# A Mamba-2 mixer's group loop: product banks evacuated into SBUF, its queues reordered

## The chip, the cores and the metric

The kernel runs on one core of a Trainium2 chip as one program. The time is the device time in microseconds. The core's engines are TensorE (PE: matmuls, PEld: its weight loads), VectorE (DVE), ScalarE (ACT), GpSimd (POOL) and SyncE (SP, which only issues transfers). Each works through its own queue of instructions in order; between engines they wait on semaphores. TensorE reads from SBUF and writes to the eight banks of PSUM, 128 partitions of 512 fp32 numbers each.

## The reference

Three blocks on 512 tokens of width 1024, all in fp32: a block with a short convolution and an FFN, a block with a Mamba-2 mixer and an FFN, and a block of windowed and sparse attention with an FFN. The change touches the mixer alone:

```python
z, xbc, dt_raw = split(h @ w_in)
xbc = silu(causal_depthwise_conv(xbc, conv_w) + conv_b)          # width 4
xs, bm, cm = split(xbc)                                           # 8 groups
dt = softplus(dt_raw + dt_bias);  a = -exp(a_log)
y = ssd(xs, dt, a, bm, cm) + d_skip * xs
y = rms_normalize_per_group(y * silu(z)) * norm_g
return y @ w_out
```

`ssd` is, for each head, y_t = C_t h_t with h_t = exp(dt_t a) h_(t-1) + dt_t B_t x_t^T. A group has 4 heads of 64 columns, and B and C of 128 columns that its heads share.

## The kernel before

Every large product is made in three matmuls of single-pass fp32 pieces: a weight chunk of 128x1024 is loaded into one of 4 ring slots (`raw`), ScalarE rounds it to its high part (`whi`, L1103), GpSimd subtracts to get the low part (`wlo`, L514), and TensorE multiplies high by high, high by low and low by high (L553). A chunk is 24 matmuls of 128x512.

The mixer runs group by group. While group g is scanned, the projections of group g + 1 run. The scan takes its quadratic form: with S the running sums of dt times a, the product for a head is (C B^T, masked, times exp(S_l - S_s)) times (dt x). One round of the loop, `m_body(g)`, holds on each engine:

- TensorE: six projection chunks of group g + 1; between them `ssd_turn` (8 transpositions of x, banks 4 and 5), `ssd_sum` (the sum of squares over the partitions for the norm of group g - 1, by a product with ones, bank 7), `ssd_cb` (C B^T, banks 4, 5 and 6) and `ssd_y` twice (half f = 0 into bank 7, f = 1 into bank 6).
- VectorE: `conv` of the four parts of group g + 1 (s = 0, 1 for x, 2 for B, 3 for C; four operations each, L1721 and L1723), `scaled_x` (dt x, L1908), `group_sum` (adds the squares of the two halves, L1891), `segment` (S_l - S_s cut at 0, L1918), `masked_cb` (L1924), `decayed` (exponential times C B^T, L1933), `group_norm` (reciprocal L1896, two products L1898) and `epilogue` (adds D x, L1882, and multiplies with silu(z), L1886) for each half.
- ScalarE: `split_next` (the roundings L1103), `ssd_exp` (three exponentials L1273 and one L1275 for each head), `copy_cb` (the copies L1282 and L1283 out of banks 5 and 6), `group_root` (L1291), `conv_silu` (L1257: xg twice, bg, cg), `gate_silu` (L1263) and `group_square` (L1287). Exponential, root and silu each need another table, so that a change between them is a table load.

The order on each engine is the order in which these calls stand in the code; nothing moves them. `grp_ready` counts the silu results of a group's four parts, `y_done` the products of `ssd_y`, `yt_done` the finished halves of the epilogue, `gacc` the added squares, `gsum` their sum on TensorE, `gstd` the roots, `cbm_act` the copies.

Behind the seventh round stands the last group, written out: while it is scanned, TensorE begins the output product `m_out` from the groups that are normalized already (`out_high`, `out_low`, `out_part`). ScalarE and VectorE split each normalized tile into `m_hi` (L1330) and `m_lo` (L1564), in the calls `mixed(first, last)`.

## Time and profile before

| | |
|---|---|
| time, median of 3 runs | 2211.74 us (2209.34 to 2215.78) |
| the profiled execution's own time | 2215.78 us |
| its span, from the first to the last instruction | 2213.9 us |
| TensorE busy | 2173.9 us, 98% |
| VectorE busy | 1200.6 us, 54% |
| ScalarE busy | 999.4 us, 45% |
| GpSimd busy | 972.5 us, 44% |
| TensorE's granted clock, mean | 0.983 |

The busy time of an engine is the union of its instructions. Matmuls are pipelined: each row's duration (0.39 us for a 128x512 one) is longer than the distance between two starts, so the starts tell more than the durations. An idle time in brackets names who released the instruction.

### The profile page before, as it was taken

Reading aid. Unit: us, or ns where it says so; the run is one execution under the profiler, and the core shown is the slowest. Engines: PE = TensorE matmul, PEld = TensorE weight load, DVE = VectorE, ACT = ScalarE, POOL = GpSimd, SP = SyncE. Lnnn points to the kernel's source line nnn. Section 1 sums busy time; section 2 is a strip of 40 time slices with the busy share of each in tenths; the row PEclk is TensorE's granted clock in tenths of the full one; section 3 lists DMA queues with packets and bytes.
Section 4 is the critical chain, followed back from the end, with each engine's and each line's share of the span. In section 5 each row is a group of like instructions: output and inputs, shape, how many; then the busy total and the mean of one; then the engine's idle time right before and its main releaser. Section 6 shows DMA issues by size and latency. Waiting matters only on the chain.

```text
span 2213.9 us, 29018 instructions
## 1 busy us (share of the span) xinstructions
PE 2173.9 (98%) x10458; PEld 1762.6 (80%) x10458; DVE 1200.6 (54%) x1719; ACT 999.4 (45%) x1425; POOL 972.5 (44%) x421
## 2 busy tenths in 40 slices
PE   7999999999999999999999999999999999999998
PEld 5788888888878777778888888888777688888886
DVE  5876665521176877876522221240888745666512
ACT  4324543334445655654543434453555644444432
POOL 3544444346644333334544456556122143444563
PEclk8999999999999999999999999999999899999999
DMA  7653475553315344333233223344221132333232
GB/s 316 220 209 124 159 275 204 189 155 96 119 49 192 115 147 157 114 124 103 69 99 100 93 76 94 108 122 156 85 70 45 33 105 81 107 97 95 78 95 74
DMA packets 74337, 273.88 MB, mean 124 GB/s; under 512 B 8631, under 2 KB 11319, under 8 KB 67848
## 3 DMA queue, kind: packets, MB, share of 16 engines
q1 hardware_dynamic: 70872, 266.77, 36.4%
q10 hardware_dynamic: 3376, 5.90, 0.8%
q8 instruction: 58, 0.95, 0.2%
q14 instruction: 31, 0.25, 0.0%
HBM read 269.24 MB, written 8.12 MB: 125 GB/s over the span
## 4 chain that ended last, share of the span: by engine, by line
PE 76%; issue 13%; POOL 5%; DVE 4%; ACT 1%; DMA 1%; ACTq 0%; SPq 0%; POOLq 0%; DVEq 0%
PE bank L553 60%; POOL wlo L514 5%; PE bank L973 4%; PE bank L1065 2%; PE bank L576 1%; PE bank L1030 1%; PE bank L994 1%; PE bank L618 1%; PE bank L1013 1%; PE bank L626 1%; PE bank L580 1%; PE bank L665 1%; DMA ada_first<-ada_d 1%; DVE x L1623 1%; DVE bank L1686 1%
## 5 line engine op out<-in xcount | busy, mean ns | idle before, releaser
L514 POOL TENSOR_TENSOR wlo<-raw,whi 128x1024 fp32r<-128x1024 f32 x382 | 927.0, 2434 | 1150.0 <-ACT whi L1103 1149.7
L1103 ACT ACTIVATE whi<-raw 128x1024 fp32r<-128x1024 f32 x382 | 400.6, 1055 | 560.4 <-PE bank L553 537.0
L553 PE MATMUL bank<-h_hi,whi 128*128 128x512 f32 x1608 | 633.0, 394 | 1.9 <-POOL wlo L514 1.9
L553 PE MATMUL bank<-h_hi,wlo 128*128 128x512 f32 x1608 | 626.5, 390 | 0.0
L553 PE MATMUL bank<-h_lo,whi 128*128 128x512 f32 x1608 | 625.8, 389 | 0.0
L553 PEld LDWEIGHTS bank<-h_hi,whi 128*128 128x128 f32 x1608 | 301.9, 188 | 68.0 <-issue 6.3
L553 PEld LDWEIGHTS bank<-h_hi,wlo 128*128 128x128 f32 x1608 | 301.8, 188 | 64.3
L553 PEld LDWEIGHTS bank<-h_lo,whi 128*128 128x128 f32 x1608 | 302.0, 188 | 61.5
L553 PE MATMUL bank<-g_hi,whi 128*128 128x512 f32 x592 | 230.4, 389 | 0.0
L553 PE MATMUL bank<-g_hi,wlo 128*128 128x512 f32 x592 | 230.3, 389 | 0.0
L553 PE MATMUL bank<-g_lo,whi 128*128 128x512 f32 x592 | 230.3, 389 | 0.0
L1785 DVE TENSOR_TENSOR tb<-ta,bank 128x512 f32<-128x512 f32 x44 | 30.2, 686 | 210.1 <-PE bank L553 193.4
L1564 DVE TENSOR_TENSOR g_lo<-tb,g_hi 128x512 f32 (+1 forms) x52 | 108.2, 2081 | 51.9 <-ACT g_hi L1235 45.0
L553 PEld LDWEIGHTS bank<-g_lo,whi 128*128 128x128 f32 x592 | 111.1, 188 | 23.2
L553 PEld LDWEIGHTS bank<-g_hi,whi 128*128 128x128 f32 x592 | 111.1, 188 | 23.0
L553 PEld LDWEIGHTS bank<-g_hi,wlo 128*128 128x128 f32 x592 | 111.1, 188 | 23.0
L1580 DVE TENSOR_TENSOR sums<-sums,sq 128x512 f32<-128x512 f32 x21 | 14.5, 692 | 186.2 <-ACT sq L1166 186.1
L1723 DVE SCALAR_TENSOR_TENSOR tb<-bank,vec,tb 128x511 f32<-128x511 f32 (+1 forms) x140 | 104.9, 749 | 9.8
L576 PE MATMUL bank<-h_hi,whi 128*128 128x512 f32 x160 | 67.2, 420 | 10.4 <-ACT h_hi L1148 10.4
L529 POOL TENSOR_TENSOR h_lo<-tb,h_hi 128x512 fp32r<-128x512 f32 x35 | 45.2, 1293 | 67.2 <-ACT tb L1149 66.8
L576 PE MATMUL bank<-h_hi,wlo 128*128 128x512 f32 x160 | 66.2, 414 | 0.0
L2153 DVE TENSOR_TENSOR x<-x,bank 128x512 f32<-128x512 f32 x8 | 5.5, 688 | 86.4 <-PE bank L553 86.4
(359 smaller groups left out, 2994.5 us busy)
## 6 DMA issues: line engine op xcount, KB each, us to landing
raw<-f_in_d SPq DMA_DIRECT2D x88, 512.0 KB, 3.5
raw<-m_d SPq DMA_DIRECT2D x65, 512.0 KB, 3.6
ada_f<-ada_d SPq DMA_DIRECT2D x24, 1024.0 KB, 6.7
raw<-g_in_d SPq DMA_DIRECT2D x44, 512.0 KB, 3.5
raw<-w_in_d SPq DMA_DIRECT2D x41, 512.0 KB, 3.5
csb<-cs_d SPq DMA_DIRECT2D x32, 640.0 KB, 6.1
ada_a<-ada_d SPq DMA_DIRECT2D x16, 1024.0 KB, 4.9
raw<-a_in_d SPq DMA_DIRECT2D x24, 512.0 KB, 5.9
```

What stands on the lines that cost most here:

```text
L514: nc.gpsimd.tensor_tensor(wlo[:, s], raw[:, s], whi[:, s].bitcast(F32), ALU.subtract).then_inc(lo_ready, 1)
L529: nc.gpsimd.tensor_tensor(h_lo[:, k, :], tb[:, k % 2, :], h_hi[:, k, :].bitcast(F32), ALU.subtract).then_inc(in_ready, 1)
L553: mm = nc.tensor.matmul(psum[bank][:], w[:, s, kk, :], xs[part == "lo"][:, k, :], start=first and kk == 0 and i == 0, stop=last and kk == ...
L576: nc.tensor.matmul(psum[tiles[i]][:], w[:, (C0[name] + i) % RING, k, :], h_hi[:, k, :], start=k == 0 and j == 0, stop=False)
L580: mm = nc.tensor.matmul(psum[tiles[i]][:], whi[:, (C0[name] + i) % RING, k, :], h_lo[:, k, :], start=False, stop=k == KD - 1)
L618: mm = nc.tensor.matmul(psum[bank][:, i:i + 1], src[:, i * P:(i + 1) * P], ones[:, 0:1], start=start and i == 0, stop=False, skip_group_ch ...
L973: mm = nc.tensor.matmul(psum[7][:], w[:, c % RING, m // 3, :], (h_hi, h_lo)[part == "lo"][:, m // 3, :], start=m == 0, stop=m == 23)
L1065: mm = nc.tensor.matmul(psum[b][:], w[:, c % RING, k, :], (h_hi, h_lo)[part == "lo"][:, k, :], start=kk == 0 and i == 0, stop=kk == 3 and ...
L1103: nc.scalar.activation(whi[:, s], raw[:, s], ACT.Copy).then_inc(hi_ready, 1)
L1564: TT(dst, whole, hi.bitcast(F32), ALU.subtract).then_inc(in_ready, 1)
L1723: ins = STT(out=out[:, d:S], in0=src[:, 0:S - d], scalar=col(width - 1 - d), in1=out[:, d:S], op0=ALU.mult, op1=ALU.add)
L1785: TT(tb[:, j % 2, :], ta[:, j % 2, :], psum[b][:], ALU.mult).then_inc(bank_free[b], 1)
```

## The change

The second operand of the epilogue changes its place: its first operation writes into `ta` in SBUF instead of back into the PSUM bank, and a new semaphore `y_evac` counts it; TensorE waits for `y_evac` where it waited for `yt_done` before it writes banks 6 and 7 again. `ssd_turn` waits for all four parts of the next group, where it waited for two and `ssd_cb` for the rest. The last group's sum of squares goes into bank 6 (`group_bank`), as one product over squares that VectorE has added, where TensorE had added them in two products. On ScalarE and VectorE several calls change places. The diff, without its first hunk that only declares the semaphore:

```diff
--- before
+++ after
@@ -276,6 +276,10 @@
             sem(n) for n in ("score_done", "soft_done", "pexp_done", "pn_done", "tr_done", "pt_done", "pv_done"))
 
         block = ctx.enter_context(nc.Block())
+
+        def group_bank(g):
+
+            return 7 if g < GROUPS - 1 else 6
 
         def tile(t, j):
 
@@ -741,11 +745,11 @@
             def ssd_sum(g):
 
                 pe.wait_ge(gacc, g + 1)
-                nc.tensor.matmul(psum[7][:], ones[:], sq[:, 0, :], start=True, stop=True).then_inc(gsum, 1)
+                nc.tensor.matmul(psum[group_bank(g)][:], ones[:], sq[:, 0, :], start=True, stop=True).then_inc(gsum, 1)
 
             def ssd_turn(g, p):
 
-                pe.wait_ge(grp_ready, 4 * g + 2)
+                pe.wait_ge(grp_ready, 4 * (g + 1))
                 for f in range(2):
                     for i in range(NT):
                         mm = nc.tensor.transpose(psum[4 + f][:, i * P:(i + 1) * P], xg[:, p, f, i * P:(i + 1) * P], ident)
@@ -754,7 +758,6 @@
             def ssd_cb(g, p):
 
                 pe.wait_ge(xdt_done, 2 * (g + 1))
-                pe.wait_ge(grp_ready, 4 * (g + 1))
                 for i in range(NT):
                     nc.tensor.matmul(psum[4][:, i * P:(i + 1) * P], bg[:, p, i * P:(i + 1) * P], cg[:, p, i * P:(i + 1) * P],
                                      start=True, stop=True)
@@ -773,7 +776,7 @@
                 if f:
                     pe.wait_ge(cbm_act, 2 * (g + 1))
                 elif g:
-                    pe.wait_ge(yt_done, 2 * g - 1)
+                    pe.wait_ge(y_evac, 2 * g - 1)
                 bank = psum[7 - f]
                 for i in range(NT):
                     for off in range(1 + (i in OFF_COL)):
@@ -798,7 +801,7 @@
                 project(1)
                 if g:
                     ssd_sum(g - 1)
-                    pe.wait_ge(yt_done, 2 * g)
+                    pe.wait_ge(y_evac, 2 * g)
                 ssd_cb(g, p)
                 project(2)
                 project(3)
@@ -874,7 +877,7 @@
             ssd_turn(g, g % 2)
             out_high(1)
             ssd_sum(g - 1)
-            pe.wait_ge(yt_done, 2 * g)
+            pe.wait_ge(y_evac, 2 * g)
             ssd_cb(g, g % 2)
             out_high(2)
             for m in range(3):
@@ -885,10 +888,7 @@
             ssd_y(g, 1)
             out_part(0, near - 2, near)
             out_part(1, CH, near)
-            for f in range(2):
-                pe.wait_ge(gsq_out, 2 * g + f + 1)
-                mm = nc.tensor.matmul(psum[7][:], ones[:], sq[:, f, :], start=f == 0, stop=f == 1)
-            mm.then_inc(gsum, 1)
+            ssd_sum(g)
             out_part(2, CH, near)
             out_part(3, CH, near)
             for m in range(4):
@@ -1288,18 +1288,20 @@
 
             def group_root(g):
                 act.wait_ge(gsum, g + 1)
-                nc.scalar.activation(rstd[:], psum[7][:], ACT.Sqrt, bias=epscol[:], scale=1.0 / 256).then_inc(gstd, 1)
+                nc.scalar.activation(rstd[:], psum[group_bank(g)][:], ACT.Sqrt, bias=epscol[:], scale=1.0 / 256).then_inc(gstd, 1)
 
             def m_body(g):
 
                 G = g + 1
+                if g:
+                    group_square(g - 1, 1)
                 split_next(G, 0)
                 ssd_exp(g, 0)
-                copy_cb(g)
                 ssd_exp(g, 1)
                 split_next(G, 1)
                 if g:
                     group_root(g - 1)
+                copy_cb(g)
                 ssd_exp(g, 2)
                 ssd_exp(g, 3)
                 conv_silu(G, 0)
@@ -1317,11 +1319,9 @@
                     return
                 group_square(g, 0)
                 conv_silu(G, 3)
-                gate_silu(G, 0)
-                split_next(G, 4)
-                group_square(g, 1)
-                gate_silu(G, 1)
-                split_next(G, 5)
+                for f in range(2):
+                    gate_silu(G, f)
+                    split_next(G, 4 + f)
 
             def mixed(first, last):
 
@@ -1346,9 +1346,9 @@
             copy_cb(g)
             ssd_exp(g, 2)
             ssd_exp(g, 3)
+            mixed(8, 12)
+            group_root(g - 1)
             split_hi(C0["m_out"] + RING)
-            group_root(g - 1)
-            mixed(8, 12)
             split_hi(C0["m_out"] + RING + 1)
             mixed(12, 14)
             split_hi(C0["m_out"] + RING + 2)
@@ -1879,11 +1879,12 @@
 
                 p = g % 2
                 dve.wait_ge(y_done, 2 * g + f + 1)
-                step(STT(out=psum[7 - f][:], in0=xg[:, p, f], scalar=V("m_d", 2 * g + f), in1=psum[7 - f][:],
-                         op0=ALU.mult, op1=ALU.add))
+                STT(out=ta[:, f, :], in0=xg[:, p, f], scalar=V("m_d", 2 * g + f), in1=psum[7 - f][:],
+                    op0=ALU.mult, op1=ALU.add).then_inc(y_evac, 1)
+                dve.wait_ge(y_evac, 2 * g + f + 1)
 
                 read_out(T0["m_in"] + 1 + GSTEP * g + 4 + f)
-                TT(ta[:, f, :], psum[7 - f][:], zg[:, p, f], ALU.mult).then_inc(yt_done, 1)
+                TT(ta[:, f, :], ta[:, f, :], zg[:, p, f], ALU.mult).then_inc(yt_done, 1)
 
             def group_sum(gi):
 
@@ -1945,15 +1946,15 @@
                     scaled_x(g)
                 segment(g, 0)
                 segment(g, 1)
+                conv(G, 1)
                 masked_cb(g)
                 decayed(g, 0)
                 decayed(g, 1)
-                conv(G, 1)
                 segment(g, 2)
                 segment(g, 3)
+                conv(G, 2)
                 decayed(g, 2)
                 decayed(g, 3)
-                conv(G, 2)
                 if g:
                     group_norm(g - 1)
                 conv(G, 3)
@@ -1980,13 +1981,14 @@
             decayed(g, 1)
             segment(g, 2)
             segment(g, 3)
+            mixed(8, 12)
             decayed(g, 2)
             decayed(g, 3)
-            mixed(8, 12)
             group_norm(g - 1)
             mixed(12, 14)
             for f in range(2):
                 epilogue(g, f)
+            group_sum(g)
             group_norm(g)
             mixed(14, 16)
             residual_sums("m_out", 2, y_m, sums_m)
```

Two places show the new order. The first is on ScalarE in the middle of a round. Names: csb are the decays of a head, cbm the masked product, whi the rounded weight chunk, rstd the root. Before:

```order
L1275 ACTIVATE csb<-csb 128x512 [waits seg_done]
L1282 ACTIVATE cbm<-bank 128x512 [waits m_done,cb_done]
L1283 ACTIVATE cbm<-bank 128x256
L1273 ACTIVATE csb<-csb,ncs_tok 128x384 [waits csb_in1]
L1273 ACTIVATE csb<-csb,ncs_tok 128x128
L1273 ACTIVATE csb<-csb,ncs_tok 128x256
L1275 ACTIVATE csb<-csb 128x512 [waits seg_done]
L1103 ACTIVATE whi<-raw 128x1024 [waits chunk_done,raw_in0]
L1291 ACT_TABLE_LOAD
L1291 ACTIVATE rstd<-bank,epscol 128x512 [waits gsum]
L1273 ACT_TABLE_LOAD
```

And now:

```order
L1275 ACTIVATE csb<-csb 128x512 [waits seg_done]
L1273 ACTIVATE csb<-csb,ncs_tok 128x384 [waits csb_in1]
L1273 ACTIVATE csb<-csb,ncs_tok 128x128
L1273 ACTIVATE csb<-csb,ncs_tok 128x256
L1275 ACTIVATE csb<-csb 128x512 [waits seg_done]
L1103 ACTIVATE whi<-raw 128x1024 [waits chunk_done,raw_in2]
L1291 ACT_TABLE_LOAD
L1291 ACTIVATE rstd<-bank,epscol 128x512 [waits gsum]
L1282 ACTIVATE cbm<-bank 128x512 [waits m_done,cb_done]
L1283 ACTIVATE cbm<-bank 128x256
L1273 ACT_TABLE_LOAD
```

The two copies into cbm have moved from behind the first head's exponential to behind the root; the exponentials of the second head stand ahead of them now. The number of table loads is the same.

The second is on VectorE, in the last group, behind its segments. Names: m_lo are the low halves of normalized tiles, ta the epilogue's two halves, sq the squares. Before:

```order
L1933 TENSOR_TENSOR csb<-csb,cbm 128x1280 [waits exp_done] x2
L1564 TENSOR_TENSOR m_lo<-y32,m_hi 128x512 [waits in_hi] x4
L1896 RECIPROCAL rstd<-rstd 128x512 [waits gstd]
L1898 SCALAR_TENSOR_TENSOR y32<-ta,vec,rstd 128x512 [waits dve_step]
L1898 SCALAR_TENSOR_TENSOR y32<-ta,vec,rstd 128x512
L1564 TENSOR_TENSOR m_lo<-y32,m_hi 128x512 [waits in_hi] x2
L1882 SCALAR_TENSOR_TENSOR bank<-xg,vec,bank 128x512 [waits y_done]
L1886 TENSOR_TENSOR ta<-bank,zg 128x512 [waits bank_free3,dve_step]
L1882 SCALAR_TENSOR_TENSOR bank<-xg,vec,bank 128x512 [waits y_done]
L1886 TENSOR_TENSOR ta<-bank,zg 128x512 [waits bank_free0,dve_step]
L1896 RECIPROCAL rstd<-rstd 128x512 [waits gstd]
```

And now:

```order
L1564 TENSOR_TENSOR m_lo<-y32,m_hi 128x512 [waits in_hi] x4
L1934 TENSOR_TENSOR csb<-csb,cbm 128x1280 [waits exp_done] x2
L1897 RECIPROCAL rstd<-rstd 128x512 [waits gstd]
L1899 SCALAR_TENSOR_TENSOR y32<-ta,vec,rstd 128x512 [waits dve_step]
L1899 SCALAR_TENSOR_TENSOR y32<-ta,vec,rstd 128x512
L1564 TENSOR_TENSOR m_lo<-y32,m_hi 128x512 [waits in_hi] x2
L1882 SCALAR_TENSOR_TENSOR ta<-xg,vec,bank 128x512 [waits y_done]
L1887 TENSOR_TENSOR ta<-ta,zg 128x512 [waits bank_free3,y_evac]
L1882 SCALAR_TENSOR_TENSOR ta<-xg,vec,bank 128x512 [waits y_done]
L1887 TENSOR_TENSOR ta<-ta,zg 128x512 [waits bank_free0,y_evac]
L1892 TENSOR_TENSOR sq<-sq 128x512 [waits gsq_out]
L1897 RECIPROCAL rstd<-rstd 128x512 [waits gstd]
```

Four of the subtractions into m_lo stand ahead of the last two decays, both epilogues write and then read ta, and an addition of squares has come in between the epilogues and the last reciprocal.

## Rows read from the trace of the kernel before

**Rows 1.** Busy time by stretch: from:to, us, PE, PEld, DVE, ACT, POOL, PEclk, DMA share, GB/s.
```profile
630.00:1010.00 380.00, 378.11 (x1989) 301.25 (x1988) 287.96 (x430) 219.55 (x334) 138.51 (x57) 1.00 0.38 131
```

**Rows 2.** Waits, 630 to 1010: who for whom, us in total, times, longest us.
```profile
DVE bank L1882 <- PE bank L788: 14.9, 8, 6.5
...
PE bank L553 <- POOL wlo L514: 1.9, 2, 1.4
```

**Rows 3.** Timeline of TensorE in a round: start us, us, what, idle before.
```profile
747.48 1.04 PE L751 MATMUL bank<-kst,xg 128*128 128x128 f32 x8
...
753.84 1.02 PE L744 MATMUL bank<-sq,ones 128*128 128x512 f32 x2
...
789.27 1.03 PE L751 MATMUL bank<-kst,xg 128*128 128x128 f32 x8
```

**Rows 4.** Timeline of ScalarE in a round.
```profile
757.09 0.60 ACT L1282 ACTIVATE cbm<-bank 128x512 f32<-128x512 f32 x1 [0.51 <-PE bank L764]
...
760.64 1.28 ACT L1291 ACT_TABLE_LOAD   x1
...
761.93 0.69 ACT L1291 ACTIVATE rstd<-bank,epscol 128x512 f32<-128x512 f32 x1
...
763.94 1.31 ACT L1273 ACTIVATE csb<-csb,ncs_tok 128x384 f32<-128x384 f32 x3
...
765.15 0.62 ACT L1275 ACTIVATE csb<-csb 128x512 f32<-128x512 f32 x1
...
782.56 0.63 ACT L1287 ACTIVATE sq<-ta 128x512 f32<-128x512 f32 x1 [8.12 <-DVE ta L1886]
...
783.10 0.71 ACT L1257 ACTIVATE cg<-tb,vec 128x512 f32<-128x512 f32 x1
...
783.71 0.58 ACT L1263 ACTIVATE zg<-bank 128x512 f32<-128x512 f32 x1
```

**Rows 5.** Timeline of VectorE in a round.
```profile
758.09 3.10 DVE L1933 TENSOR_TENSOR csb<-csb,cbm 128x1280 f32<-128x1280 f32 x2 [0.31 <-ACT cbm L1283]
...
761.12 0.74 DVE L1721 TENSOR_SCALAR tb<-bank,vec 128x512 f32<-128x512 f32 x1
...
764.12 1.66 DVE L1918 TENSOR_SCALAR csb<-csb,cs_tok 128x128 f32<-128x128 f32 x8
...
772.65 3.34 DVE L1896 RECIPROCAL rstd<-rstd 128x512 f32<-128x512 f32 x1
...
776.03 2.10 DVE L1898 SCALAR_TENSOR_TENSOR y<-ta,vec,rstd 128x512 f32<-128x512 f32 x2
...
781.06 0.74 DVE L1882 SCALAR_TENSOR_TENSOR bank<-xg,vec,bank 128x512 f32<-128x512 f32 x1
...
781.84 0.69 DVE L1886 TENSOR_TENSOR ta<-bank,zg 128x512 f32<-128x512 f32 x1
...
791.55 2.07 DVE L1891 TENSOR_TENSOR sq<-sq 128x512 f32<-128x512 f32 x1
```

**Rows 6.** Timelines of GpSimd and VectorE where they meet.
```profile
790.66 2.41 POOL L514 TENSOR_TENSOR wlo<-raw,whi 128x1024 fp32r<-128x1024 f32 x1 [0.61 <-ACT whi L1103]
...
959.44 3.73 POOL L514 TENSOR_TENSOR wlo<-raw,whi 128x1024 fp32r<-128x1024 f32 x1 [11.90 <-ACT whi L1103]
...
958.45 2.49 DVE L1564 TENSOR_TENSOR m_lo<-y,m_hi 128x512 fp32r<-128x512 f32 x4
```

**Rows 7.** Timelines of ScalarE, TensorE and GpSimd at the end of the last group.
```profile
969.37 1.05 ACT L1103 ACTIVATE whi<-raw 128x1024 fp32r<-128x1024 f32 x1
...
979.16 0.50 PE L821 MATMUL bank<-m_hi,whi 128*128 128x512 f32 x1
...
985.40 2.40 POOL L514 TENSOR_TENSOR wlo<-raw,whi 128x1024 fp32r<-128x1024 f32 x1 [0.48 <-ACT whi L1103]
...
986.08 0.63 ACT L1287 ACTIVATE sq<-ta 128x512 f32<-128x512 f32 x1 [0.76 <-DVE ta L1886]
...
990.03 1.88 PE L890 MATMUL bank<-sq,ones 128*128 128x512 f32 x4
```

4 lines of the change are left out of this document (2 added, 2 removed).

## The prediction, made before the changed kernel was run

> **What bounds the kernel now.** I read four views, in this order. First the table of busy time by stretch [rows 1]: the change lies wholly in the mixer stage, from 630 to 1010 us, and there TensorE is busy for 378.1 of 380 us at a granted clock of 1.00, while VectorE has 288, ScalarE 220 and GpSimd 139. Then the waits of that stage [rows 2]: TensorE waited for others in 2 places, 1.9 us in all, and both times for the low half of a weight chunk; VectorE waited 14.9 us for TensorE's output products, so it is the one with time to spare. Then TensorE's timeline [rows 3]: the transpositions of two neighbouring groups start at 747.48 and 789.27, so a group costs 41.79 us, and within it TensorE goes from one operation to the next without a gap. Last the timelines of ScalarE, VectorE and GpSimd over one group [rows 4 to 6]: they show how early each thing is ready that TensorE asks for.
>
> So a wait that the change removes elsewhere buys nothing unless TensorE stood in it, and it did not. The change can win only TensorE's own work or the 1.9 us. It loses as soon as something comes later than TensorE asks for it.
>
> **Part 1: one matmul less.** For the last group TensorE summed the squares with two 128x512 fp32 matmuls. The four pieces of these took 1.88 us from 990.03 [rows 7]; the two pieces of the one product that a group has elsewhere took 1.02, from 753.84 [rows 3]. The difference, 0.86, is what TensorE no longer does; I take 0.8. The pieces overlap, so the ends are 0.4 (half) and 1.0 (a whole product).
>
> **Part 2: evacuation into SBUF, y_evac for yt_done.** The epilogue's first operation now writes ta instead of its bank and releases the bank itself, 0.7 us sooner than the second did (row 781.84 in [rows 5]). Nobody on TensorE waited for that release [rows 2], so this is worth 0. Its price is that the second operation now reads two SBUF tiles. Such an operation of VectorE and a subtraction of GpSimd don't overlap here: the addition of squares at 791.55 took 2.07 us, where the multiplication of the same size at 781.84 took 0.69, because GpSimd ran from 790.66 to 793.07, and GpSimd's row of 959.44 took 3.73 instead of 2.41 because VectorE had a pair of SBUF tiles in each operation up to 960.94 [rows 5, 6]. The old multiplication had one operand in PSUM. Inside the loop the new one falls into a gap of GpSimd; at the end of the stage it doesn't (part 4). Bounds for one multiplication: 0 and 2.4 us more.
> The Trainium skill, page "SBUF — State Buffer", section "Who interferes with whom", says the same of an instruction with two SBUF inputs against a GpSimd one that reads SBUF, and adds that whichever issues first holds the ports while the other is blocked. In row 959.44 GpSimd asked in the middle of four back-to-back VectorE operations and got in only behind the fourth, so among queued neighbours the trace does not follow the issue order. What the page's order would give is rival 1.
>
> **Part 3: the loop's new order.** ScalarE now does the root before it copies the masked-product banks, and squares the second half last, behind both weight splits; VectorE does one convolution ahead of the masked product, the next one between segments 2, 3 and decays 2, 3; TensorE transposes only when all four parts of the next group are there. I lay the new order from rows of before. Start at the end of the first epilogue, 0. ScalarE's operations overlap by a tenth (the square of 0.63 starts at 782.56, cg at 783.10), so steps count from start to start: square 0.54, cg 0.61, zg 0.5, split 1.05 (row 969.37 in [rows 7]): 2.7 [rows 4]. GpSimd then has two splits back to back, 2.41 each [rows 6]: 7.6. Behind them VectorE's addition of squares ends, 0.6: 8.2. Convolution 3.0 (761.12 to 764.12), one segment 0.9: 12.1. ScalarE: an exponential of 0.5, three of 1.2, one of 0.5, split 1.07, table load 1.29, root 0.70, copies until VectorE starts 1.0 (757.09 to 758.09): 18.3. VectorE: two decays 2.8 (the row of 3.10 holds 0.2 of waiting), segment 0.8: 21.9. ScalarE: exponentials 0.5, 1.2, 0.6, table load 1.3, silu 0.7: 26.2. VectorE: convolution 3.0, 0.9 behind GpSimd, two decays 2.8, reciprocal 3.38, two products 1.4, convolution 3.0, epilogue 1.4: 42.1.
> The lap is 42.1 against TensorE's 41.8, where it had been loose before. It is covered by the spare time. In the old order cg is ready at 783.8 and the transposition starts at 789.27: 5.4 us. Laid from the end of the addition at 793.6 in the new order (3.0 + 0.9 + 6.2 + 3.6 + 4.3 + 15.9, the pieces above), the next first epilogue ends at about 827.5; by the old order it ends at 781.84 + 0.69 + 41.79 = 824.3. So cg is 3.2 to 3.6 later and the spare is about 2 us; each of the four laps that follow takes 0.35 of it, and 0.6 is left at the last group. So the loop costs TensorE 0. Without that cover it costs 0.35 a group and what the first lap overran.
>
> **Part 4: the end of the stage.** VectorE's epilogue is some 4 us late there; of this 1.3 is what it had waited for TensorE's product (14.9 us in 8 such waits, [rows 2], most of them shorter than the mean), so it enters the last group 2.7 us late. Its masked product still waits mostly for TensorE's scores, so 0.7 of that remains; the first decay then sits behind the GpSimd split that has slid there (+1.4), which makes 2.2. ScalarE splits the next output chunk only after four roundings, the table load and the root (instead of right behind the exponentials, 969.37): 2.2 of lag, 2.05 for four roundings, 1.3 and 0.7 put it at 975.6; GpSimd waits there for the decays to end at 977.4 and its low half is ready at 979.8, and TensorE asks at 979.16 (the row behind its first output product in [rows 7]), a few tenths later for its own lag. Stall 0.4. VectorE reaches the reciprocal 1.8 us late (4 roundings and 2 decays in either order), its products meet the split (+1.4), so the two roundings behind end 3.1 late. The first epilogue's multiplication meets the next split (1.9 more; it would have been 0.7), the second's then ends at 990.0, so the square behind it, which started at 986.08 [rows 7], is over at 990.7. New here: VectorE's addition of the two squares, which asks just behind the start of the last split (2.4 long, as row 985.40), so it ends at about 993.4. TensorE asks at 990.03 + 0.4 = 990.5 and stands 3.0 us. What hangs behind (root, reciprocal, last two tiles) has 1 us in hand and shifts with it. TensorE's longest wait of the stage, 1.4 for a low half [rows 2], has its cause behind this point (the first output tile's evacuation) and stays.
> Bounds for this part: 0, if no multiplication meets a split (by the old timing the addition is done at 986.08 + 0.63 + 0.69 = 987.4, well ahead of 990.03), and 5 to 6, if all of them meet one at its start and the spare of the last transposition (0.6) and of the row sum is gone.
>
> **Sum.** -0.8 + 0 + 0 + 0.4 + 3.0 = +2.6 us. The profiled execution took 2215.78 us (span 2213.9, so 1.9 around it): 2218.4 for it, and on the median of 2211.74, 2214.3 us.
>
> **Rivals.**
> 1. The loop falls behind TensorE (slower). Mechanism: GpSimd gets in between decays 2 and 3 and VectorE loses another 2.4 us there. That is more than the spare of 2, so TensorE waits at the transposition from the second lap on, 0.35 in each of 6 (2.0), in the last group for the row sum and the scaled inputs (0.65 + 0.35), for the root 0.5, for the split 1.8, at the new addition 3.1: 8.5, less 0.8: +7.7, 2219.4. It decides from a lag of 2 us per group on. For: all operations there have two SBUF inputs, and the lap is 0.3 over. Against: row 959.44. Chance 0.20.
> By the page's order of issue named in part 2 this is what would happen.
> 2. The stage's end doesn't stall: the splits fall into other gaps, and only the matmul is gone: -0.8, 2210.9. For: three collisions have to come together, and a shift of 2 us undoes two. Against: the splits are issued by ScalarE right beside the very squares. Chance 0.15.
> 3. It is faster by more than the noise: TensorE's gapless rows hide a stretch in which matmuls wait for a bank, and the earlier release frees it. Against: [rows 1] leave 1.9 us of idle time in the stage, and [rows 2] name all of it. It would need 7 us, one in each group: 2204. Chance 0.04.
> The forecast itself: 0.61.
>
> **How the numbers follow.** 0.3%, 6.6 us, is about what a measurement of this kernel can tell from no change. The forecast and rival 2 are within it. Rival 1 is just over it on the slow side, and I count three quarters of its chance (0.15) and 0.05 of the forecast's upper tail as slower: 0.20. Faster: rival 3 and a little for the spread of 6.4 us among the runs shown: 0.05. Same: 0.75. Range: from rival 2 less the spread of a median, 2208.5, to rival 1 with 2 us for longer handovers, 2221.5.
>
> **What would show it.** Right: TensorE's interval between transpositions stays 41.79; idle time of TensorE before the last row sum of about 3 us, put down to VectorE; the last epilogue's multiplication longer than 2 us; cg done 1 to 2 us ahead of the transpositions, less in each group. Wrong: idle time before the transpositions (rival 1), none before the row sum (rival 2), a group shorter than 41.79 (rival 3).

## The result, and the profile after

Over four runs of each kernel in turn, the changed kernel took 2225.59 us (median; 2222.69 to 2228.93) and the kernel before 2212.89. The ratio is 1.0056, with a 95% interval from 1.0037 to 1.0076: 12.7 us slower. The forecast was 2214.3, with a range up to 2221.5. The profiled execution took 2225.32 us (span 2223.4; before, 2213.9).

Three numbers of the trace carry what follows: the **interval** from the transposition of one group to that of the next; the **end**, from the start of the last transposition to that of the first matmul on sums_m; and what TensorE waited for in between. Before, the interval is 41.79 and the end 96.03, by these rows:

```profile
954.60 1.03 PE L751 MATMUL bank<-kst,xg 128*128 128x128 f32 x8
...
1050.63 1.62 PE L618 MATMUL bank<-ones,sums_m 128*128 128x1 f32 x14
```

The mixer stage of the changed kernel, by stretch (the answer to [rows 1]):

```profile
630.00:1023.00 393.00, 380.13 (x1983) 300.56 (x1982) 310.12 (x431) 217.68 (x333) 140.51 (x57) 1.00 0.37 127
```

Its waits of TensorE over the same stretch (the answer to the second row of [rows 2]): who for whom, us in total, times, longest us.

```profile
PE bank L755 <- ACT cg L1257: 7.4, 6, 1.4
PE bank L748 <- DVE sq L1892: 2.5, 2, 2.3
PE bank L557 <- POOL wlo L518: 1.9, 2, 1.4
PE bank L824 <- POOL wlo L518: 0.9, 1, 0.9
PE bank L762 <- DVE xdt L1909: 0.2, 1, 0.2
```

TensorE is busy for 380.1 of 393 us, where it was for 378.1 of 380, and VectorE's busy time rises from 288 to 310 although it has only one operation more of 0.7 us: operations of VectorE have become longer. Six transpositions wait for cg, and the sum of squares waits once 2.3 for the new addition.

TensorE's timeline of the changed kernel, at three transpositions, at the last group's sum of squares and at the end of the stage (start, us, what, idle before):

```profile
746.30 1.09 PE L755 MATMUL bank<-kst,xg 128*128 128x128 f32 x8 [0.36 <-ACT cg L1257]
...
789.70 1.09 PE L755 MATMUL bank<-kst,xg 128*128 128x128 f32 x8 [1.41 <-ACT cg L1257]
...
961.50 1.09 PE L755 MATMUL bank<-kst,xg 128*128 128x128 f32 x8 [1.36 <-ACT cg L1257]
...
1001.27 1.54 PE L748 MATMUL bank<-sq,ones 128*128 128x512 f32 x2 [2.27 <-DVE sq L1892]
1001.83 1.40 PE L824 MATMUL bank<-m_hi,whi 128*128 128x512 f32 x1
...
1005.45 0.40 PE L824 MATMUL bank<-m_lo,whi 128*128 128x512 f32 x1
...
1062.72 1.50 PE L622 MATMUL bank<-ones,sums_m 128*128 128x1 f32 x13
```

The interval is 43.40 (746.30 to 789.70). The first transposition stands at 663.13 and the last at 961.50, 298.4 us apart (before: 664.83 and 954.60, 289.8), and the end is 101.22 (961.50 to 1062.72). So the loop lost 8.6 us and the end 5.2, 13.8 in the stage. The medians differ by 12.7. The two profiled executions differ by only 9.5 in span, because outside the stage the changed one was 4.3 us shorter: 1.7 ahead at the first transposition, and 2.6 behind the stage, where its mean granted clock was 0.99 against 0.98. The change touches nothing there, and no run ties that difference to it; so the stage is compared, not the span.

VectorE's timeline of the changed kernel in one round (the answer to [rows 5]):

```profile
787.68 0.69 DVE L1887 TENSOR_TENSOR ta<-ta,zg 128x512 f32<-128x512 f32 x1
...
797.04 3.11 DVE L1919 TENSOR_SCALAR csb<-csb,cs_tok 128x128 f32<-128x128 f32 x8
...
805.59 2.89 DVE L1934 TENSOR_TENSOR csb<-csb,cbm 128x1280 f32<-128x1280 f32 x2 [1.83 <-ACT cbm L1283]
808.40 1.65 DVE L1919 TENSOR_SCALAR csb<-csb,cs_tok 128x128 f32<-128x128 f32 x8
813.79 0.75 DVE L1721 TENSOR_SCALAR tb<-bank,vec 128x512 f32<-128x512 f32 x1 [3.74 <-ACT xg L1257]
...
816.81 5.88 DVE L1934 TENSOR_TENSOR csb<-csb,cbm 128x1280 f32<-128x1280 f32 x2
822.61 3.34 DVE L1897 RECIPROCAL rstd<-rstd 128x512 f32<-128x512 f32 x1
...
831.10 0.69 DVE L1887 TENSOR_TENSOR ta<-ta,zg 128x512 f32<-128x512 f32 x1
```

ScalarE's in the same round (the answer to [rows 4]):

```profile
804.01 0.69 ACT L1291 ACTIVATE rstd<-bank,epscol 128x512 f32<-128x512 f32 x1
804.59 0.59 ACT L1282 ACTIVATE cbm<-bank 128x512 f32<-128x512 f32 x1
```

GpSimd's in the same round (the answer to the first row of [rows 6]):

```profile
791.15 7.54 POOL L518 TENSOR_TENSOR wlo<-raw,whi 128x1024 fp32r<-128x1024 f32 x3 [13.24 <-ACT whi L1103]
802.77 2.40 POOL L518 TENSOR_TENSOR wlo<-raw,whi 128x1024 fp32r<-128x1024 f32 x1 [4.09 <-ACT whi L1103]
815.33 2.41 POOL L518 TENSOR_TENSOR wlo<-raw,whi 128x1024 fp32r<-128x1024 f32 x1 [10.15 <-ACT whi L1103]
818.68 2.66 POOL L518 TENSOR_TENSOR wlo<-raw,whi 128x1024 fp32r<-128x1024 f32 x1 [0.95 <-ACT whi L1103]
```

The row at 816.81 is the one to look at. Decays 2 and 3 take 5.88 us where decays 0 and 1, the same size, take 2.89. GpSimd's third split (815.33; the chunks of a group are counted from the one at 796, the last of the three in the first row) would be over at 817.74 and holds decay 2; the fourth (818.68) asks while decay 2 still runs, and runs at once behind it (2.66 us, 2.40 when alone), so decay 3 waits for it. VectorE's next row of consequence is the first epilogue's multiplication, at 787.68 and at 831.10: the lap is 43.42, and TensorE's interval follows it.

### The profile page after: what moved, and what is told of

It reads as the page before. It is cut to its first block, busy times and chain, and to the rows that moved or that the text cites. A ratio compares the mean times of both kernels' runs of the same rounds, so it can differ in the third digit from the quotient of the medians.

```text
span 2223.4 us, 29014 instructions
## 1 busy us (share of the span) xinstructions
PE 2169.3 (98%) x10456; PEld 1756.8 (79%) x10456; DVE 1220.1 (55%) x1720; ACT 997.9 (45%) x1425; POOL 974.2 (44%) x421
## 4 chain that ended last, share of the span: by engine, by line
PE 75%; issue 14%; POOL 5%; DVE 4%; ACT 1%; DMA 1%; ACTq 0%; SPq 0%; POOLq 0%; DVEq 0%
PE bank L557 60%; POOL wlo L518 4%; PE bank L973 4%; PE bank L1065 2%; PE bank L580 2%; PE bank L994 1%; PE bank L1030 1%; PE bank L622 1%; PE bank L1013 1%; PE bank L630 1%; PE bank L669 1%; DMA ada_first<-ada_d 1%; PE bank L584 1%; DVE x L1623 1%; DVE bank L1686 1%
## 5 line engine op out<-in xcount | busy, mean ns | idle before, releaser
L1934 DVE TENSOR_TENSOR csb<-csb,cbm 128x1280 f32<-128x1280 f32 x32 | 68.8, 2191 | 11.5 <-ACT cbm L1283 11.4
```

What stands on the lines that cost most here:

```text
L1934: TT(csb[:, r, :], csb[:, r, :], cbm[:], ALU.mult).then_inc(m_done, 1)
```

## The experiments

Intervals, ends and waits are from one profiled execution each, the medians and ratios from the timed runs beside the kernel before; "waits" are TensorE's, without the 1.9 in two places for low halves that every kernel has, and without sums of 0.3 or less.

| kernel | median, ratio [95%] | interval | end | TensorE's waits |
|---|---|---|---|---|
| before | 2212.9 | 41.79 | 96.03 | none |
| after | 2225.6, 1.0056 [1.0037, 1.0076] | 43.4 | 101.22 | turns 7.4, sum 2.3, split 0.9 |
| dec_first | 2213.8, 1.0010 [1.0001, 1.0020] | 41.79 | 96.65 | sum 1.3 |
| fused | 2217.7, 1.0021 [1.0011, 1.0031] | 41.79 | 99.22 | sum 2.3, split 0.8 |
| cb_first | 2226.5, 1.0066 [1.0049, 1.0083] | 43.6 | 101.12 | turns 7.9, sum 2.3, split 0.8 |
| turn_wait | 2225.2, 1.0064 [1.0047, 1.0081] | 41.79, then 43.4 | 102.03 | sums 5.2, products 3.2, first output product 0.6 |
| halves | 2229.3, 1.0063 [1.0041, 1.0086] | 43.6 | 101.40 | turns 9.3, sum 2.3, products 1.4, split 1.0 |
| evac_only | 2214.1, 1.0004 [0.9994, 1.0014] | 41.79 | 96.04 | none |
| old_end | 2221.6, 1.0034 [1.0022, 1.0047] | 43.4 | 96.98 | turns 7.7 |
| new_end | 2210.2, 0.9987 [0.9977, 0.9996] | 41.79 | 95.15 | none |
| one_sum | 2210.0, 0.9993 [0.9983, 1.0003] | 41.79 | 95.15 | none |
| dec_last | 2216.4, 1.0014 [1.0004, 1.0023] | 41.79 | 98.10 | a group's sum 1.5 |
| new_end_sbuf | 2213.4, 1.0002 [0.9990, 1.0013] | 41.79 | 96.15 | sum 0.7 |
| dec_psum | 2211.1, 0.9988 [0.9978, 0.9998] | 41.79 | 95.15 | none |
| diff_f32 | one run, 2216.7 | 41.79 | 97.36 | split 1.3, sum 0.6 |
| prod_inplace | one run, 2212.8 | 41.79 | 97.35 | split 1.3, sum 0.6 |
| diff_behind | one run, 2220.8 | 43.0 | 97.95 | turns 6.3, sum 0.6 |

### Which part of the loop costs the time

**dec_first**, the decays back ahead of the convolution:

```diff
-                conv(G, 2)
                 decayed(g, 2)
                 decayed(g, 3)
+                conv(G, 2)
```

> The changed kernel with decays 2 and 3 back ahead of the third convolution. Theory 1 (the place of the decays: behind the convolution they meet GpSimd's splits, which get in before decay 2 and between 2 and 3): both decays take about 2.9 us instead of 5.9 and overlap the wait for ScalarE, the lap falls below TensorE's 41.79, the waits at the transpositions (7.4 us) are gone, the whole about 8 us faster than the changed kernel. Theory 2 (ScalarE's order, root ahead of the copies and square last, makes the lap): the interval stays above 42.5. Theory 3 (the wait for four parts by itself): it stays 43.4.

Measured: interval 41.79, no wait in the loop, the stage 13.2 us shorter than in the changed kernel; that is more than the 8 expected, since the end came back as well (96.65). VectorE in the round of 787.82:

```profile
806.65 1.49 DVE L1934 TENSOR_TENSOR csb<-csb,cbm 128x1280 f32<-128x1280 f32 x1
808.37 1.49 DVE L1934 TENSOR_TENSOR csb<-csb,cbm 128x1280 f32<-128x1280 f32 x1 [0.23 <-ACT csb L1275]
810.48 0.75 DVE L1721 TENSOR_SCALAR tb<-bank,vec 128x512 f32<-128x512 f32 x1 [0.62 <-ACT xg L1257]
...
830.68 1.29 DVE L1909 TENSOR_TENSOR xdt<-bank,dt_tok 128x512 f32<-128x512 f32 x2 [5.08 <-PE bank L755]
```

The decays take 1.49 each, stand partly in the time in which VectorE had waited for ScalarE's silu (3.74 in the changed kernel, 0.62 here), and behind them there is idle time of 5 us again. Theories 2 and 3 fall: both things they name are still in this kernel.

**fused**, both decays in one instruction at the changed place:

```diff
-                decayed(g, 2)
-                decayed(g, 3)
+                dve.wait_ge(exp_done, HPG * g + 4)
+                TT(csb[:, 2:4, :], csb[:, 2:4, :], cbm[:].unsqueeze(1).broadcast_to([P, 2, PACK]),
+                   ALU.mult).then_inc(m_done, 2)
```

> The changed kernel with decays 2 and 3 as one VectorE instruction over both rows, in the same place. It leaves GpSimd no seam to get into. Theory 1: the pair takes 2.8 to 3.4 us instead of 5.9 (its start may still be held by a split under way), the lap is about 41, and the waits at the transpositions are gone or under 0.2 us each; about 7 us faster than the changed kernel. Theory 2 or 3: interval still 43.4.

VectorE's timeline of fused at that place, and GpSimd's:

```profile
816.00 3.61 DVE L1957 TENSOR_TENSOR csb<-csb,cbm 128x2560 f32<-128x2560 f32 x1
```

```profile
814.52 2.41 POOL L518 TENSOR_TENSOR wlo<-raw,whi 128x1024 fp32r<-128x1024 f32 x1 [10.16 <-ACT whi L1103]
817.88 3.99 POOL L518 TENSOR_TENSOR wlo<-raw,whi 128x1024 fp32r<-128x1024 f32 x1 [0.95 <-ACT whi L1103]
```

The pair takes 3.61 instead of 5.88, and it is GpSimd whose row grows, to 3.99. The seam was worth 2.3 us a lap, and without it the interval is 41.79: it alone decides whether the loop holds. The other 0.7 (3.61 against 2.89) is the split that was under way. The stage is 10.6 us shorter than in the changed kernel.

**cb_first**, the copies back ahead of the root:

```diff
                 ssd_exp(g, 0)
+                copy_cb(g)
                 ssd_exp(g, 1)
...
-                copy_cb(g)
```

> The changed kernel with the two copies of the masked-product banks back behind the first exponentials, ahead of the root. Theory 1: VectorE saves the 1.8 us that it stood for the copies, no more, and the decays 2 and 3 still take 5.9: interval 41.8 to 42.2, waits of 0.0 to 0.4 at the transpositions. Theory 2: the interval is 41.79 and the lap well below it, and the decays 2 and 3 are back at 2.9 because everything stands 1.8 us earlier. Theory 3: 43.4.

Theories 1 and 2 are both wrong here: nothing was gained (43.6). The number comes nearest to theory 3, which dec_first excludes. VectorE's timeline of cb_first in a round, and GpSimd's:

```profile
805.68 4.87 DVE L1934 TENSOR_TENSOR csb<-csb,cbm 128x1280 f32<-128x1280 f32 x2
...
818.89 5.87 DVE L1934 TENSOR_TENSOR csb<-csb,cbm 128x1280 f32<-128x1280 f32 x2
```

```profile
805.41 2.39 POOL L518 TENSOR_TENSOR wlo<-raw,whi 128x1024 fp32r<-128x1024 f32 x1 [4.83 <-ACT whi L1103]
```

VectorE no longer waits 1.83 for the copies, but decays 0 and 1 now come up just behind the start of GpSimd's second split and take 4.87 instead of 2.89. The wait became a collision of the same size.

**turn_wait**, the transposition waiting for two parts:

```diff
-                pe.wait_ge(grp_ready, 4 * (g + 1))
+                pe.wait_ge(grp_ready, 4 * g + 2)
...
+                pe.wait_ge(grp_ready, 4 * (g + 1))
                 pe.wait_ge(xdt_done, 2 * (g + 1))
```

> The changed kernel with the transposition waiting for two parts of the group and the scores for all four, as before. Theory 3 (the earlier wait is the loss): all of the loop's 8.6 us come back. Theory 1 (the lap runs over VectorE, ScalarE and GpSimd alone and is 43.4 whatever TensorE waits for): the first laps run at 41.79 on the 5.4 us between transposition and scores, and when 4 laps of 1.6 have used them up TensorE waits at the scores instead, 1 to 3 us in all; the whole is 5 to 6 us faster than the changed kernel, and VectorE's own interval stays above 43.

Theory 3 falls, and of theory 1 the size: the interval stays 41.79 only up to the fourth transposition, because the sum of squares and the y products come late as well (behind it up to 0.45 for the sum and 0.7 for the products of a group, 1.8 for the sum in the last one). VectorE's own lap is 43.45, as theory 1 has it, but the stage is only 1.2 us shorter, not 5 to 6. The wait of the diff is where the delay shows, not where it is made.

**dec_last**, the kernel before with the one move:

```diff
-                decayed(g, 2)
-                decayed(g, 3)
                 conv(G, 2)
+                decayed(g, 2)
+                decayed(g, 3)
```

> The kernel before with one move alone: decays 2 and 3 behind the third convolution. Theory 1: they meet the same two splits, the pair takes 5 to 6 us, and VectorE's way from transposition to the next first epilogue grows by 5 to 6 us, which is what it had in hand: interval between 41.79 and 42.3, and where TensorE waits, it waits for y products or scores, under 1 us a group. If the other moves of the loop are what makes it slow, nothing changes at all: the pair stays at 3 us. The end of the stage stays within 1 us of 96.03.

The pair takes 5.87. The first epilogue's multiplications stand at 785.85 and 827.95: a lap of 42.10, a third of a microsecond over TensorE's, and until the last group this is eaten from the spare time; the end pays 2.1, where it was expected to stay within 1. Between this and 43.4 are 1.3. By the rows they come from the 1.83 that VectorE waits for the copies in ScalarE's new order: from that multiplication to the end of segments 0 and 1 both kernels take 12.5 us, to the end of segments 2 and 3 20.9 here and 22.4 in the changed kernel; no run isolates it, since in cb_first a collision took its place. Each of the two moves alone leaves the loop at 41.79 (dec_first has ScalarE's new order, dec_last the decays' new place); together they break it.

### The end of the stage

**old_end**, the changed kernel with the last group of before, and **new_end**, the kernel before with the last group of the change (its edit, of which old_end is the reverse; its part on TensorE is the one shown under one_sum):

```diff
...
-            split_hi(C0["m_out"] + RING)
-            group_root(g - 1)
             mixed(8, 12)
+            group_root(g - 1)
+            split_hi(C0["m_out"] + RING)
...
+            mixed(8, 12)
             decayed(g, 2)
             decayed(g, 3)
-            mixed(8, 12)
...
+            group_sum(g)
             group_norm(g)
```

> The changed kernel with the last group as before (order on ScalarE and VectorE, two matmuls for the sum). The loop stays as it is (interval 43.4). Last transposition to the last row sum, 96.03 before and 101.22 after. Theory A (the last group's own new order and its addition of squares cost the 5.2): 96 to 97.5, no wait for sq over 0.5, no stretch at a lower clock behind it. Theory B (VectorE's lag out of the loop costs it): 99 or more.

> The kernel before with the last group's part of the change alone: its order on ScalarE and VectorE, the addition of squares and one matmul. Interval 41.79. Last transposition to last row sum: theory A 98 to 101, with a wait of about 2 us for the addition; theory B (on time, the addition is ready before TensorE asks) 95.2, which is 96.03 less one matmul, 0.86.

old_end goes by theory A (96.98), new_end by theory B (95.15, 0.88 less than before). So the last group's part is harmless, even a gain, when VectorE comes on time, and costs 4.2 us when it comes late. Neither theory alone was right.

**one_sum**, of that part only the addition and the single matmul:

```diff
-            for f in range(2):
-                pe.wait_ge(gsq_out, 2 * g + f + 1)
-                mm = nc.tensor.matmul(psum[7][:], ones[:], sq[:, f, :], start=f == 0, stop=f == 1)
-            mm.then_inc(gsum, 1)
+            ssd_sum(g)
...
+            group_sum(g)
             group_norm(g)
```

> The kernel before with only the addition of the last group's squares and one matmul for their sum, all orders as before. The last square ends at 986.71; the addition can be held by GpSimd until 987.80 and takes 0.7, so it is done by 988.5, and TensorE asks at 990.03: no wait, last transposition to last row sum 95.2 (0.86 less than before), the whole 0.9 us faster, which the comparison cannot tell from nothing.

As expected: 95.15.

**evac_only** and **new_end_sbuf**, the epilogue into SBUF on the kernel before and on new_end:

```diff
...
-                    pe.wait_ge(yt_done, 2 * g - 1)
+                    pe.wait_ge(y_evac, 2 * g - 1)
...
-                step(STT(out=psum[7 - f][:], in0=xg[:, p, f], scalar=V("m_d", 2 * g + f), in1=psum[7 - f][:],
-                         op0=ALU.mult, op1=ALU.add))
+                STT(out=ta[:, f, :], in0=xg[:, p, f], scalar=V("m_d", 2 * g + f), in1=psum[7 - f][:],
+                    op0=ALU.mult, op1=ALU.add).then_inc(y_evac, 1)
+                dve.wait_ge(y_evac, 2 * g + f + 1)
...
-                TT(ta[:, f, :], psum[7 - f][:], zg[:, p, f], ALU.mult).then_inc(yt_done, 1)
+                TT(ta[:, f, :], ta[:, f, :], zg[:, p, f], ALU.mult).then_inc(yt_done, 1)
```

> The kernel before with nothing but the epilogue into SBUF and TensorE's waits on y_evac. Forecast by part 2 of the prediction: nothing; interval 41.79, stage 385.8 us as before, at most 0.5 more at its end. Theory 4 (two SBUF operands meet GpSimd and cost the lap): the lap of before has 5 us in hand, so here too the interval stays 41.79, but VectorE's second epilogue multiplication takes over 1.5 us in some rounds.

> The kernel before with the last group's part and the epilogue into SBUF, the loop's order as before. Interval 41.79. Theory E (the second epilogue operation, reading two SBUF tiles, meets the split and makes the addition of squares late): it takes 2.4 instead of 0.7 us, the addition meets the last split as well, TensorE waits 0.5 to 1.3 us for it, last transposition to last row sum 95.8 to 96.6. Rival (only the loop's lag makes it late): no wait, 95.15 as without the SBUF part.

Alone it costs nothing. In the loop its multiplication stays at 0.69 (781.83; 1.03 once, in the first round), so theory 4 falls there; in the last group it takes 2.44 (at 983.00), and nothing of TensorE hangs on that while the squares are not added first. On new_end the end grows by 1.00, as theory E has it. VectorE's timeline of new_end_sbuf, at the multiplication and the addition of squares:

```profile
983.78 2.46 DVE L1884 TENSOR_TENSOR ta<-ta,zg 128x512 f32<-128x512 f32 x1
...
988.41 2.47 DVE L1889 TENSOR_TENSOR sq<-sq 128x512 f32<-128x512 f32 x1 [0.79 <-ACT sq L1284]
```

**dec_psum**, the edit of dec_first and the reverse of the one just shown, on the changed kernel:

> The changed kernel with decays 2 and 3 back ahead of the third convolution and the epilogue back through its bank; everything else of the change kept. Theory E: the multiplication no longer meets the split (0.7 instead of 2.5 us), the addition of squares is done before TensorE asks, last transposition to last row sum 95.15, stage 384.9: 0.9 us faster than the kernel before. Rival (the wait of 1.26 us there comes from ScalarE's and VectorE's order in the last group): it stays about 1, and the stage is 386.

VectorE's timeline of dec_psum at the same two operations:

```profile
983.80 0.69 DVE L1886 TENSOR_TENSOR ta<-bank,zg 128x512 f32<-128x512 f32 x1
...
986.67 2.47 DVE L1891 TENSOR_TENSOR sq<-sq 128x512 f32<-128x512 f32 x1 [0.78 <-ACT sq L1287]
```

Through the bank the multiplication at 983.80 takes 0.69 (2.46 in new_end_sbuf at 983.78, beside the same split), the second square ends 1.7 us sooner, and TensorE does not wait, although the addition still meets a split. This kernel and new_end are the two that beat the kernel before: both by 0.9 us in the stage, as measured by 0.12% (0.02 to 0.22) and 0.13% (0.04 to 0.23). one_sum's stage is as short, but its interval contains 1; the measured differences are larger than the 0.9 us of the stage, and the rest of them is not explained.

### Why GpSimd got in

**halves**: decays 2 and 3 as two instructions each:

```diff
-                TT(csb[:, r, :], csb[:, r, :], cbm[:], ALU.mult).then_inc(m_done, 1)
+                if r < 2:
+                    TT(csb[:, r, :], csb[:, r, :], cbm[:], ALU.mult).then_inc(m_done, 1)
+                else:
+                    for at in (0, PACK // 2):
+                        ins = TT(csb[:, r, at:at + PACK // 2], csb[:, r, at:at + PACK // 2], cbm[:, at:at + PACK // 2], ALU.mult)
+                    ins.then_inc(m_done, 1)
```

> The changed kernel with decays 2 and 3 as two VectorE instructions of 640 columns each (four in a row, about 0.75 us apiece, like the four 0.6 us subtractions that kept GpSimd out at 959.44). Theory L (a short operation is followed by the next before GpSimd gets in, a 1.4 us one is not): VectorE is held only at the start, the four take about 4 us, GpSimd's fourth split is the one that grows, interval 41.79 or up to 0.2 more. Theory W (length does not matter, GpSimd gets in at the first seam behind its request): the four take 5.9 to 6.2 and the interval stays 43.4 or more.

VectorE's timeline of halves, the four pieces:

```profile
819.26 6.00 DVE L1938 TENSOR_TENSOR csb<-csb,cbm 128x640 f32<-128x640 f32 x4
```

Theory W: length does not keep it out. In the last group of the same kernel the same four instructions run at full speed, and GpSimd, which asks during the third (11.05 us behind its last split), goes behind the fourth:

```profile
988.03 3.02 DVE L1938 TENSOR_TENSOR csb<-csb,cbm 128x640 f32<-128x640 f32 x4
```

```profile
990.19 3.08 POOL L518 TENSOR_TENSOR wlo<-raw,whi 128x1024 fp32r<-128x1024 f32 x1 [11.05 <-ACT whi L1103]
```

**prod_inplace**, four products more in the last group of dec_psum, ahead of mixed(4, 8); **diff_f32** has the subtraction `y32[:, k, :]` less `m_hi[:, k, :]` into the same four buffers instead:

```diff
+            for k in range(4, 8):
+                s = (tb[:, 0, :], tb[:, 1, :], zg[:, 0, 0], zg[:, 0, 1])[k - 4]
+                dve.wait_ge(in_hi, I0["m_out"] + k + 1)
+                TT(s, s, m_hi[:, k, :].bitcast(F32), ALU.mult).then_inc(diff_out, 1)
             mixed(4, 8)
```

> The kernel dec_psum with four more subtractions on VectorE in the last group, ahead of the ones that make m_lo of tiles 4 to 7: same operation, same operands, same size, but fp32 outputs into free buffers. GpSimd's split asks about 1 us behind their start. Theory R (the output type decides: only operations that write fp32r keep GpSimd out): it gets in behind the second, so these four take 2.4 more than the 2.5 that four m_lo take, about 4.6 to 4.9 us, and GpSimd's row is about 2.7 long. Theory S (any such back-to-back subtractions keep it out): the eight run through in 4.9 us together and GpSimd's row is about 6.2 long. The rest of the stage within 1 us of dec_psum's.

> The kernel dec_psum with four more operations on VectorE at the same place of the last group as in diff_f32, but of the decays' kind: multiplications in place, fp32, 512 columns, of free buffers. GpSimd's split asks about 1 us behind their start, as there. Theory I (what lets GpSimd in between decays is their kind, a product written over its own operand): it gets in behind the second of them, the four take 4.6 to 4.9 us instead of 2.5, GpSimd's row is about 2.7 long. Theory H (it is the history: in the loop GpSimd asks 0.95 us behind its last split, here 13 us behind it): the eight run through in 4.9 us and GpSimd's row is about 6.2.

The same in both: 6.18 us for GpSimd's row. VectorE's timeline of prod_inplace, and GpSimd's:

```profile
960.21 1.29 DVE L1980 TENSOR_TENSOR tb<-tb,m_hi 128x512 f32<-128x512 f32 x2
...
962.62 2.49 DVE L1564 TENSOR_TENSOR m_lo<-y,m_hi 128x512 fp32r<-128x512 f32 x4
...
965.74 4.38 DVE L1933 TENSOR_TENSOR csb<-csb,cbm 128x1280 f32<-128x1280 f32 x2
```

```profile
961.20 6.18 POOL L518 TENSOR_TENSOR wlo<-raw,whi 128x1024 fp32r<-128x1024 f32 x1 [13.02 <-ACT whi L1103]
```

GpSimd asks at 961.20 and gets in when all eight are over (6.18 long). Theories R and I fall. The stage is 2.2 us longer than dec_psum's in both, where diff_f32's expectation had at most 1.

**diff_behind**: on dec_psum, four subtractions more, like those that kept it out, where the changed kernel has its decays:

```diff
                 conv(G, 2)
+                if g > 1:
...
+                    for k in range(4):
+                        TT(m_lo[:, 12 + k, :], y32[:, 0, :], y32[:, 1, :], ALU.subtract).then_inc(diff_out, 1)
```

> The kernel dec_psum with four subtractions of 512 columns with fp32r output (on tiles not yet made) on VectorE in each round from the third on, directly behind the third convolution, where the changed kernel has its decays: GpSimd's third split is still running when they come up, and it asks for the fourth 0.95 us behind its end, in the middle of the four. Theory H (GpSimd gets in at the next seam when it asks just behind a split that had held VectorE, whatever operations stand there): the four take 2.5, 0.9 held at the start and 2.1 to 2.4 in the middle, 5.4 to 5.8 us, and GpSimd's row is 2.4 to 2.8. Theory K (subtractions of this kind keep it out anywhere): about 3.4 us, and GpSimd's row is 3.5 to 4.

VectorE's timeline of diff_behind, and GpSimd's:

```profile
816.73 5.47 DVE L1961 TENSOR_TENSOR m_lo<-y 128x512 fp32r<-128x512 f32 x4
```

```profile
815.25 2.40 POOL L518 TENSOR_TENSOR wlo<-raw,whi 128x1024 fp32r<-128x1024 f32 x1 [10.15 <-ACT whi L1103]
818.60 2.45 POOL L518 TENSOR_TENSOR wlo<-raw,whi 128x1024 fp32r<-128x1024 f32 x1 [0.95 <-ACT whi L1103]
```

The four take 5.47 us instead of 2.49, and GpSimd's second row is 2.45 long: theory H. The same kind of operation keeps GpSimd out in one place and not in the other. This kernel's interval is 43.03, with a wait of 1.04 at three transpositions and of 3.17 at the last: 5.5 us more on VectorE at this point break the loop too. How much of that the collisions are (3.0 of the 5.5) was not separated.

The kernel before has it as well, behind the loop, where VectorE adds up the row sums of the output:

```profile
1004.48 2.37 POOL L514 TENSOR_TENSOR wlo<-raw,whi 128x1024 fp32r<-128x1024 f32 x1 [16.68 <-ACT whi L1103]
1007.24 2.43 POOL L514 TENSOR_TENSOR wlo<-raw,whi 128x1024 fp32r<-128x1024 f32 x1 [0.39 <-ACT whi L1103]
```

```profile
1004.98 2.41 DVE L1580 TENSOR_TENSOR sums_m<-sums_m,sq 128x512 f32<-128x512 f32 x1 [1.47 <-ACT sq L1166]
1007.32 2.90 DVE L1585 TENSOR_TENSOR ta<-x,y_m 128x512 f32<-128x512 f32 x1
```

The split of 1004.48 holds the addition; the next one asks 0.39 us behind it, while the addition ends, and gets in ahead of the multiplication, which takes 2.90 (0.69 at 1002.82). So the trace that the prediction was read from held both behaviours, inside the stretch of [rows 1].

## Why the prediction was wrong

- **Part 1** (one matmul less, 0.8): right. new_end and one_sum show 0.88.
- **Part 2** (evacuation into SBUF, 0 in the loop, its price at the end): right on both. evac_only shows 0, and new_end_sbuf the price, 1.0 at the end, by the multiplication that was named. The earlier release bought nothing.
- **Part 3** (the loop's new order, 0): this is the step that failed, at its piece "convolution 3.0, 0.9 behind GpSimd, two decays 2.8". The lap starts at the end of the first epilogue, 788.37. Laid from there, segments 2 and 3 were to be done at 21.9 and VectorE's third convolution to start at 26.2; measured are 21.7 (810.05) and 25.4 (813.79). From there to the reciprocal 6.7 were laid and 8.8 passed (to 822.61): 2.1 more, for the split that got in, which the text had excluded by [rows 6], the row of 959.44. The remaining 9.2 were 9.2. So the lap is 42.1 - 0.8 + 2.1 = 43.4. There was no cover for it: the spare time was gone by the third transposition (0.36 at 746.30).
- **fused is in effect the kernel that Part 3 laid.** Without the seam VectorE's lap is 42.09 (743.86 to 785.95), and cg is ready 2.2, 1.9 and 1.6 us ahead of the transpositions from 748.00 on, then 2.1, 1.8 and, at the last one, 0.5; the prediction had 2, 0.35 less in each lap, and 0.6. Its stage is 3.2 us longer than before, against the 2.6 of the sum. So the rest of the laying held; what the forecast lacked is the one excluded collision and what follows from it.
- The reason for it was one row carried to another place. What the row shows is true (970.13 in the changed kernel again: 3.78 behind four subtractions), but in the loop GpSimd asks 0.95 us behind the end of its previous split, and there it gets in between decays, halves and subtractions alike; the rows of 1004.48 and 1007.24 in the trace before would have warned of it. The Trainium skill, page "SBUF — State Buffer", section "Who interferes with whom", says that the order of issue decides which of the two blocks the other. By that rule what happened in the loop is as expected; in prod_inplace the trace does not follow it, since six operations of VectorE started behind GpSimd's request and went first.
- **Rival 1** named this mechanism and its waits, and priced it at +7.7. It took GpSimd's 2.4 as a lag that comes once, and then charged 0.35 a lap. But it comes back in every lap, so the lap itself is longer by it: 1.6 for each interval once the spare is gone, 8.6 in the loop. (Its waits, as they stand, add up to 8.4, not 8.5.)
- **Part 4** (+0.4 at the first output chunk, +3.0 at the new addition): measured 0.86 and 2.27 in the changed kernel, by the collisions named (in the changed kernel the epilogue's multiplication at 994.15 takes 2.46, the addition at 998.79 takes 2.43). With the loop in order it is 0 and 1.26 (dec_first), so part of it was the loop's. Two things were missing. The smaller ones are waits of 0.26 and 0.17 at the sum and the scores of the last turn. The larger one is TensorE's clock behind the 2.27 wait. The changed kernel by stretches of 1 us, columns as in [rows 1]:

```profile
1002.00:1003.00 1.00, 1.00 (x2) 0.42 (x2) 0.00 (x0) 0.15 (x1) 0.00 (x0) 0.50 0.63 246
...
1004.00:1005.00 1.00, 1.00 (x4) 0.81 (x3) 1.00 (x1) 0.00 (x0) 0.00 (x0) 0.50 0.00 0
1005.00:1006.00 1.00, 1.00 (x5) 0.77 (x5) 1.00 (x1) 0.00 (x0) 0.00 (x0) 0.86 0.00 0
```

The granted clock is 0.50 from 1002 to 1005, the lower of its two levels (1.2 GHz), and 0.86 in the next: the matmuls stand 0.43 us apart instead of 0.23. From the sum's matmul to the eighth behind it 4.18 us pass (1001.27 to 1005.45), in fused, which waited as long there and kept its clock, 2.59 (994.49 to 997.08): 1.6 for the clock, by this comparison.

The sum: of 13.8 in the stage the loop has 8.6. The end's 5.2 are 3.6 for its four waits and 1.6 for the clock, less 0.9 for the matmul, and 0.9 that no row was found for (fused, with nearly the same waits and no drop of the clock, has 0.75 left over in the same way).

## What to carry to other kernels

Lay out the lap of the engines behind the bottleneck, and ask of every operation with two SBUF operands which GpSimd operation is running or asked for when it comes up, at its new place. A row that shows them getting past each other elsewhere does not say what they do there: look in the same trace for rows that show the opposite. A delay that recurs is added to the lap, not to the lag: once the lap is longer than the bottleneck's, each round costs the whole difference. And moves that are each covered by the same spare time have to be priced together.

## What the runs showed of the hardware

- VectorE's operations and a GpSimd subtraction that both read two SBUF tiles don't overlap, and the order in which they get in depends on the place. In the last group, GpSimd asks 11 to 18 us behind its last split and stays out of an unbroken row of up to eight operations (its own row is 3.1 to 6.2 us long). In the loop it asks 0.95 us behind a split that had held VectorE, and gets in at the first seam; so it does in the kernel before, 0.39 behind such a split (1007.24). The kind of operation, its length and its output type are excluded as the cause. That this history decides is the likeliest reading; whether it is the short time since the last split, or that this split had held VectorE, or another property of the place, stays open.
- The segments, which read one SBUF tile and a scalar for each partition, also stood against GpSimd: eight took 3.11 us beside three splits in a row (797.04) and 1.65 without one (808.40).
- Turned around: one instruction over both tiles has no seam (3.61 against 5.88 us).
- TensorE's clock fell to 0.50 for some 3 us in the changed kernel, cb_first and halves behind the wait of 2.3 us at the last sum, in turn_wait behind one of 1.8 at a group's sum, and in diff_behind behind one of 3.2 at the last transposition. It did not fall in fused behind the same 2.3 us, nor in dec_first, dec_last and new_end_sbuf behind 0.7 to 1.5. In the five kernels where it fell TensorE had waited in several groups before (old_end had too, but no single wait over 1.45), in these four it had not. No run separates that from chance.
